# The second mixer of a decoder stack: position bias moved from TensorE to VectorE, heads paired across row halves, GpSimd given half of the normalising, output projection regrouped

## The reference, cut to what matters

```python
proj = h @ w_in            # qa, ka, va | qb, kb, vb | qkv_c, z_c, b_c, a_c
o_a = swa_sink_attention(qa, ka, va, sinks, slopes)   # 4 heads, 2 key heads, window 128, d = 64
o_b = moba_attention(qb, kb, vb, slopes)              # 4 heads, d = 64; causal over all 512 here
#   scores = q.k * d**-0.5 - slope * (distance); masked; softmax (o_a: with a sink term); @ v
o_c = gated_delta_rule(qc, kc, vc, g, beta)           # 4 heads, d = 128, chunks of 64 tokens
#   per chunk: v_new = u - w.S ; o = q.S + a.v_new ; S = S*exp(g_last) + k'.v_new
o_c = rms_norm_2(o_c, dn_norm) * silu(z_c)
mix = concatenate([o_a, o_b, o_c]) @ w_out
x = x + rms_norm_2(mix, mix_post_norm)
```

## Time and profile before

| what | us |
|---|---|
| median of 3 runs (lowest, highest) | 2384.92 (2378.02, 2394.63) |
| the profiled execution | 2380.75 |
| its span, first to last instruction | 2379.0 |
| TensorE busy in the span | 2267.9 (95%) |
| VectorE, ScalarE, GpSimd busy | 1196.2, 894.1, 1055.0 |
| mixer's loop, first score product to the end of the last chunk's work | 1786.9 to 1893.7 |
| mixer's tail, to the first product of the output projection | 1893.7 to 1913.8 |

### The profile page before, as it was taken

How to read it: one execution, slowest core, us unless ns; L and a number is a source line. 1 busy time by engine, 2 the same in 40 slices (tenths; PEclk the granted TensorE clock), 3 DMA queues, 4 the chain that set the end, 5 groups by cost and what they waited for, 6 DMA issues and landing times.

```text
span 2379.0 us, 32320 instructions
## 1 busy us (share of the span) xinstructions
PE 2267.9 (95%) x10448; PEld 1814.8 (76%) x10448; DVE 1196.2 (50%) x1541; ACT 894.1 (38%) x1552; POOL 1055.0 (44%) x785
## 2 busy tenths in 40 slices
PE   7999999999999999999999999989998996999996
PEld 5788888888888786666787788867796664887885
DVE  7822234444432634554248323387774348888613
ACT  4244333443333434443333443334333333323322
POOL 4644445445444445554446544443300032555553
PEclk9999999999999999999999999999999998999998
DMA  3232222222222222111222222222100011232232
GB/s 122 88 106 97 97 91 96 96 97 97 97 97 97 93 97 71 54 54 36 75 86 96 99 95 97 97 94 79 63 10 1 1 62 44 88 100 94 97 106 97
DMA packets 53354, 194.45 MB, mean 82 GB/s; under 512 B 5920, under 2 KB 6176, under 8 KB 53280
## 3 DMA queue, kind: packets, MB, share of 16 engines
q1 hardware_dynamic: 52416, 190.86, 24.1%
q10 hardware_dynamic: 864, 2.59, 0.3%
HBM read 191.34 MB, written 2.10 MB: 81 GB/s over the span
## 4 chain that ended last, share of the span: by engine, by line
PE 44%; issue 36%; POOL 17%; DVE 3%; POOLq 1%; ACT 0%; DVEq 0%; ACTq 0%
POOL w_lo L561 16%; PE proj L619 12%; PE proj L621 12%; PE proj L620 12%; PE aux L764 1%; POOL pr L576 1%; PE proj L789 1%; PE aux L767 1%; PE proj L720 1%; PE proj L718 1%; PE proj L719 1%; DVE act_l L1724 1%; PE aux L775 1%; DVE small L1704 0%; PE proj L746 0%
## 5 line engine op out<-in xcount | busy, mean ns | idle before, releaser
L561 POOL TENSOR_TENSOR w_lo<-w_stage,w_hi 128x512 fp32r<-128x512 f32 x716 | 986.6, 1387 | 1227.3 <-ACT w_hi L1141 1226.7
L1141 ACT ACTIVATE w_hi<-w_stage 128x512 fp32r<-128x512 f32 x716 | 436.7, 627 | 765.4 <-PE proj L621 712.4
L619 PE MATMUL proj<-xh,w_hi 128*128 128x512 f32 x1720 | 683.4, 397 | 36.4 <-POOL w_lo L561 30.6
L620 PE MATMUL proj<-xl,w_hi 128*128 128x512 f32 x1720 | 673.6, 392 | 0.0
L621 PE MATMUL proj<-xh,w_lo 128*128 128x512 f32 x1720 | 673.4, 391 | 0.0
L619 PEld LDWEIGHTS proj<-xh,w_hi 128*128 128x128 f32 x1720 | 324.9, 189 | 125.0 <-POOL w_lo L561 46.3
L621 PEld LDWEIGHTS proj<-xh,w_lo 128*128 128x128 f32 x1720 | 324.7, 189 | 68.3
L620 PEld LDWEIGHTS proj<-xl,w_hi 128*128 128x128 f32 x1720 | 324.8, 189 | 67.7 <-issue 2.5
L619 PE MATMUL proj<-act_h,w_hi 128*128 128x512 f32 (+1 forms) x864 | 337.7, 391 | 0.6 <-POOL w_lo L561 0.6
L620 PE MATMUL proj<-act_l,w_hi 128*128 128x512 f32 (+1 forms) x864 | 337.3, 390 | 0.0
L621 PE MATMUL proj<-act_h,w_lo 128*128 128x512 f32 (+1 forms) x864 | 337.2, 390 | 0.0
(11 more groups left out here) (309 smaller groups left out, 2360.4 us busy)
## 6 DMA issues: line engine op xcount, KB each, us to landing
w_stage<-stream SPq DMA_DIRECT2D x358, 512.0 KB, 3.3
out<-x_res SPq DMA_DIRECT2D x4, 512.0 KB, 2.6
x_res<-x SPq DMA_DIRECT2D x2, 512.0 KB, 5.5
x_res<-x ACTq DMA_DIRECT2D x2, 512.0 KB, 9.5
consts_sb<-consts ACTq DMA_DIRECT2D x1, 832.0 KB, 5.4
pos_i<-pos ACTq DMA_DIRECT2D x1, 256.0 KB, 2.6
consts_sb<-consts ACTq DMA_DIRECT2D x1, 227.0 KB, 6.6
params_sb<-params ACTq DMA_DIRECT2D x1, 194.0 KB, 4.9
```

The lines of the kernel that those rows point to most:

```text
L561: pool.tensor_tensor(w_lo[:, at, :], w_stage[:, at, :], w_hi[:, at, :].bitcast(F32), ALU.subtract).then_inc(stage_free, 1)
L619: pe.matmul(o, w_hi[:, slot, cols], hi, start=(b == 0), stop=False)
L620: pe.matmul(o, w_hi[:, slot, cols], lo, start=False, stop=False)
L1141: act.activation(w_hi[:, u % RING, :], w_stage[:, u % RING, :], ACT.Copy).then_inc(hi_done, 1)
```

## The change

- The bias products and `slope_ident` go. VectorE adds the bias instead: per head one operation in place on the scores in PSUM, distances times minus slope plus score, in front of the row maximum.
- Local heads are paired across key heads, (0, 2) and (1, 3), so that the two lie on opposite row halves; the scores of a pair always take two banks. The rows of the output weight and the sinks are reordered to match.
- `values` goes key block by key block with the two heads inside.
- The scaling is split: VectorE scales head 1 ("nr"), GpSimd head 0 (`pair_scaled`) after the new step "rs". TensorE transposes head 1 first. GpSimd's weight units are cut into those ahead of the pairs and those behind.
- The reciprocal of `r_final` stands ahead of the loop, in the place of `slope_ident`.
- Tiles 0 to 2 of `mixed` are split inside the loop, as soon as their last block is there; tile 3 and the delta tiles behind. Buffers move so that `act_h` is free for it.
- The tail: the square root stands ahead of the last `turn`; the transposes of the norm, the values of pair 14, the spreads, then the values of pair 15.
- The output projection makes its first three tiles side by side, block by block (`together`), then five as before.

```diff
@@ mixer, TensorE
+                        part = slice(64 * t, 64 * t + 64)
+                        q, keys = (a_q[part, tl, :], a_kv[part, 0, :]) if tl < 2 else (b_q[part, tl - 2, :], b_k[part, tl - 2, :])
+                        mm = pe.matmul(pair_scores(k)[:, t, :], q[:, qb * P:qb * P + P], keys[:, first:first + w],
+                                       start=True, stop=True)
-                        pe.matmul(o, q[:, qb * P:qb * P + P], keys[:, first:first + w], start=True, stop=False)
-
-                        mm = pe.matmul(o, slope_ident[:, slope, :], consts2[:, dist - w:dist], start=False, stop=True)
...
-                    for t in range(2):
+                    for t in (1, 0):
+                        if t:
+                            pe.wait_ge(mix_dve, DVE_STEP["nr", k])
+                        else:
+                            pe.wait_ge(pair_scaled, k + 1)
...
-                for t in range(2):
-                    head = 2 * (tl % 2) + t
-                    at = 64 * (head // 2) if tl < 2 else P + 64 * head
-                    for kb_ in range(w // P):
+                for kb_ in range(w // P):
+                    for t, head in enumerate(pair_heads(tl)):
+                        at = 64 * t if tl < 2 else P + 64 * head
...
+                turn(PAIRS)
                 pe.wait_ge(mix_dve, DVE_STEP["orc"])
                 for blk in range(4):
                     mm = pe.transpose(banks(0)[0:4, blk * P:blk * P + P], rc[:, blk * 4:blk * 4 + 4], con("ident", P))
                 made(mm, "ornt")
+                values(PAIRS)
                 pe.wait_ge(mix_dve, DVE_STEP["orn"])
                 for h in HEADS:
                     made(pe.matmul(banks(4 + h), ...), ("ob", h))
+                values(PAIRS + 1)
+                pe.wait_ge(mix_act, ACT_STEP["mc", PAIRS - 1])
...
+                    together(of_act, lambda k: pe.wait_ge(al_done, al.n + k + 1), DT)
+                    for t in range(DT - TOGETHER):
+                        products(tile.n % BANKS, DT, of_act)
@@ mixer, VectorE
-                        link(dve.reciprocal(sums, sums))
-                        for t in range(2):
-                            ins = dve.tensor_scalar(probs[:, n % 2, t, 0:w], probs[:, n % 2, t, 0:w], sums[:, t:t + 1], None, ALU.mult)
-                        made(ins, ("nr", n))
+                        made(dve.reciprocal(sums, sums), ("rs", n))
+                        made(dve.tensor_scalar(probs[:, n % 2, 1, 0:w], probs[:, n % 2, 1, 0:w], sums[:, 1:2], None, ALU.mult), ("nr", n))
...
+                        for t, head in enumerate(pair_heads(tl)):
+                            slope = (SLOPES_SWA if tl < 2 else SLOPES_MOBA)[head]
+                            ins = dve.scalar_tensor_tensor(pair_scores(k)[:, t, :], consts2[:, dist:dist + w], -slope,
+                                                           pair_scores(k)[:, t, :], ALU.mult, ALU.add)
+                        link(ins)
                         link(dve.tensor_reduce(nmax, pair_scores(k), AX.X, ALU.max))
...
                     attend(2 * c + 1)
+                    if c in (3, 5, 7):
+                        lo_of_mixed((c - 3) // 2)
@@ GpSimd
-            lo_units(first, units - first)
+            n = n_units(phases[:phases.index("mixer") + 1]) - RING - 2 * DT + RING
+            lo_units(first, n - first)
+            for k in range(PAIRS):
+                w = pair_of(k)[3]
+                pool.wait_ge(mix_dve, DVE_STEP["rs", k])
+                pool.tensor_scalar(probs[:, k % 2, 0, 0:w], probs[:, k % 2, 0, 0:w], soft[:, k % 2, 1, 0:1], None,
+                                   ALU.mult).then_inc(pair_scaled, 1)
+            lo_units(n, units - n)
```

More of the change, by code:

```diff
@@ L210, in mixer_steps @@
         values(2 * c + 1)
[L211 to L215, removed]
-    act += ["osqrt"]
+    attend(PAIRS)
+    act += ["osqrt"]
+    turn(PAIRS)
+    pe += ["ornt"]
+    values(PAIRS)
+    pe += each("ob")
+    values(PAIRS + 1)
     dve += ["orc", "orn"] + each("on")
@@ L642, in first_tiles @@
                     return
[L643 to L650, removed]
[L651 to L657 removed]
+                together(of_x, lambda k: pe.wait_ge(xl_done, 8 * x_norms[0] + k + 1), DT)
                 stats()
@@ L1073, in hybrid_mixer @@
                     values(2 * c + 1)
-                for k in (PAIRS, PAIRS + 1):
-                    attend(k)
-                    turn(k)
-                    values(k)
+                turn(PAIRS)
                 pe.wait_ge(mix_dve, DVE_STEP["orc"])
@@ L1183, in out_tiles, with grouped_out_tiles_of_y @@
                 deviation(ahead, twice)
+            def grouped_out_tiles_of_y():
+                for t in range(DT):
+                    his(2 * TOGETHER if t == 0 else 2 if t >= TOGETHER else 0)
+                    act.wait_ge(slot_free, unit.now())
+                    square(proj[:, tile.n % BANKS, :])
+                    tile.up()
+                deviation(False)
             def out_tiles_of_y(per_tile):
@@ L1579, in out_tiles, with grouped_out_tiles_of_y @@
                 deviation(twice)
+            def grouped_out_tiles_of_y(post):
+                dve.wait_ge(slot_free, unit.now() + RING + 2 * TOGETHER)
+                for t in range(DT):
+                    b = bank(2)
+                    add_square()
+                    take(dve.tensor_scalar(y[:, t, :], b, par(post, t), None, ALU.mult))
+                deviation()
             def out_tiles_of_y(per_tile, post):
@@ L1906, in hybrid_mixer @@
                                                ALU.subtract), (f"xt{l}", h))
-                for i, slope in enumerate(SLOPES_SWA + SLOPES_MOBA):
-                    ins = dve.tensor_scalar(slope_ident[:, i, :], con("ident", P), -slope, None, ALU.mult)
-                made(ins, "slopes")
+                dve.wait_ge(std_done, stds.n)
+                link(dve.reciprocal(r_final[:, :], r_final[:, :]))
                 def attend(k):
@@ L2166, in weight_blocks @@
             tile(m, P)
+        first_out, w_out = len(out), a["w_out_2"][0]
+        w_out = np.concatenate([w_out[0:64], w_out[128:192], w_out[64:128], w_out[192:]])
         for f in range(DT):
-            tile(a["w_out_2"][0], f * P)
+            tile(w_out, f * P)
+        out[first_out:first_out + TOGETHER * DT] = [out[first_out + i * DT + k] for k in range(DT) for i in range(TOGETHER)]
     if phase == "ffn":
```

113 lines of the change are left out of this document (53 added, 60 removed).

## The result

The changed kernel takes 2369.7 us (median of 5 runs, 2364.2 to 2370.0) against 2384.9 before: ratio 0.9933, interval 0.9909 to 0.9957. The forecast was 2368 in 2354 to 2381; the gain is 15.2 us, forecast 17.3. In the profiled executions the stretch that was forecast, from the loop's first score product to the first product of the output projection, takes 115.7 us against 126.9: 11.2 gained, forecast 17.3. So the total came out closer than the stretch did, and one of the steps behind the forecast did not come out: the clock.

A forecast was written before the change was run, and what follows sets the result against it. TensorE's list bounds the kernel; a ring through four engines replaces it. Loop 90.3 and tail 8.8 us, plus 10.5 for clock and hand-overs, start the output projection 17.3 us earlier: 2384.9 - 17.3 = 2368 us, range 2354 to 2381.

The forecast's parts named there:

- a ring through four engines: Loop: waits through GpSimd, TensorE, VectorE and ScalarE set the pace, 11.3 us a chunk for local heads 256 wide.
- The first two pairs take 11.1: Loop's start: the first two pairs, ahead of chunks 1 to 6, take 11.1 us.
- The start is worth 8: Loop's start: 4 us of TensorE standing and about half of 9.1 us at the lower clock go, 8 us.
- TensorE's own work, 64 us: Loop: its length were TensorE still the bound, 106.8 - 31 - 3.5 - 8 = 64 us.
- The bias at 2 x 0.45: Loop, VectorE: bias on two heads, 0.45 us each, between 0.34 for 128 columns and 0.74 for 512.
- The values, 3.5: Loop, TensorE: values with two heads alternating over opposite column halves save 0 to 8 us, taken as 3.5.
- GpSimd's half is no gain, one engine behind the other: Scaling: GpSimd's 0.93 us against VectorE's 0.35 for 256 columns; one waits for the other, 0.35 on each chunk.
- The tail, 8.8 and 4.5 for the clock: From pair 15's scaling to the output projection: 8.8 us at full clock, plus 4.5 for running at half speed again.
- One or two falls of the clock in the loop, 4 us, and 2 for hand-overs: Loop: TensorE's waits bring one or two clock falls, 4 us; hand-overs not counted elsewhere add 2 us.
- the full-clock sum: Loop: ring links added at full clock put pair 15's scaling 90.3 us after the loop's start.
- what would prove it wrong: Loop: chunks following at 8 us, or at 13 and more, or the clock at half in more than two chunks.
- The rival of the lower clock: Lower clock spreads over the loop: chunks take 16 us, 4.7 more; with all seven 2401 us; chance 4%.

The follow-up runs named there:

- e1: Changed kernel with VectorE scaling the x tile of a chunk after the odd pair's attend instead of before it: 2352.7 us, ratio 0.9862.
- e5: Kernel before with only the reciprocal of r_final moved from chunk 0 to ahead of the loop: 2379.6 us, ratio 0.9983.
- e9: Changed kernel with the bias back on TensorE as products and the x tile scaled after the odd pair's attend: 2351.4 us, ratio 0.9873.
- e10: Changed kernel with the products with the values again going head after head: 2367.7 us, ratio 0.9938.
- e6: Changed kernel with the old tail order, square root, transposes and spreads behind the values of pairs 14 and 15: 2374.2 us, ratio 0.9959.
- e4: Changed kernel with four added products nobody reads on TensorE ahead of the wait for the scaling in all 16 turns: 2355.2 us, ratio 0.9873.
- e2: Changed kernel with the bias back on TensorE as products with a scaled identity: 2362.3 us, ratio 0.9905.
- e7: Changed kernel with x tile late, both heads scaled by VectorE, and scores of pair 2c+1 ahead of values(2c) on TensorE: 2351.5 us, ratio 0.9872.

## Why the prediction was right, and where it was not

- *TensorE's list ceases to be the bound, a ring through four engines takes over*: right. e1 moved 0.75 us a chunk on VectorE alone and shortened the loop by 9.7; the one chunk at full clock took 11.0 us against 11.2, and with the clock at 0.95 pair 15 came at 93.6 against 90.3.
- *The first two pairs take 11.1*: 11.0. *The start is worth 8*: 7.9 up to pair 13 (e5), of which 3.3 reach the end when it is made alone.
- *TensorE's own work, 64 us*: borne out by the 65 us or slightly more of e9 without its bias groups.
- *The bias at 2 x 0.45*: 0.43 for 256 columns, and 0.29 and 0.69 for 128 and 512, a little under the lower bounds of 0.34 and 0.74. The prediction says that no row has the price with PSUM in and out. One did: the mask of the first attention in the kernel before, 256 columns in place, at the 0.43 us that the bias then took.

```profile
L1703 DVE TENSOR_TENSOR aux<-aux,consts_sb 128x256 f32<-128x256 f32 x32 | 13.8, 430 | 69.6 <-PE aux L767 69.1
```

- *The values, 3.5*: real but off the ring (e10), so it was no term of the forecast's end.
- *GpSimd's half is no gain, one engine behind the other*: right in the sum. GpSimd starts 0.06 us after VectorE's scaling starts, not behind it, as the profile shows for pair 15:

```profile
1889.74 0.49 DVE L1951 TENSOR_SCALAR probs<-probs,soft 128x512 f32<-128x512 f32 x1
1889.80 1.86 POOL L600 TENSOR_SCALAR probs<-probs,soft 128x512 f32<-128x512 f32 x1 [6.55 <-DVE soft L1950]
```

  But it takes 1.86 us where it took 1.56 in the first attention, and so ends 1.92 us after VectorE's start. One behind the other would be 0.49 + 1.56 = 2.05, side by side without harm 1.62. By the Trainium skill ("SBUF — State Buffer", Who interferes with whom) one of the two blocks the other for its whole instruction, which would give the 2.05. The trace comes within 0.13 us of that, though the block shows as a longer operation and not as a later start.
- *The tail, 8.8 and 4.5 for the clock*: 14.4 in place of 13.3, 1.1 more; its order is worth 4.2 (e6).
- *One or two falls of the clock in the loop, 4 us, and 2 for hand-overs*: this step failed. Pair 15 came 11.1 us behind the full-clock sum, not 6. The chunks exceed it by 0.5, 2.7, 1.7, 3.1, 2.7, -0.2 and 0.7 us, the first pairs by nothing. The clock fell six times and was at half in parts of more than two chunks, which the prediction had named as what would prove it wrong. The rival of the lower clock had the mechanism and a price of 4.7 us a chunk; at most 3.1 was paid, since no chunk ran at half throughout. What e4 gave back, 7.8 us at a clock of 0.95, is the nearest measure of what the falls cost the loop; the forecast had 4.
- The missing 5 us of the loop and 1.1 of the tail make the first product 6.1 later than forecast (115.7 after the start against 109.6). The gain by the medians is only 2.1 short of the forecast, since the medians of both kernels also carry the 4 us by which the code ahead of the loop varies. That the total came so near is to this extent luck.

So the large edits gave little in this order: of the 11.2 us that the stretch gained (15.2 by the medians), the start and the tail's new order, both small, account for 7.5 to 12. The move of the bias took 5 us of the stretch and 7.5 of the median away again (e2). The pairing of the scores and the early split of `mixed` weren't tried alone, so what each of them is worth stays open.

**A version that beats both.** The changed kernel with the x tile behind the second `attend` (e1), 2352.7, or with the bias left on TensorE as well (e9), 2351.4. By the medians that is 17 to 18 us below the changed kernel and 32 to 33 below the one before; by the stretch, 13 to 16 and 24 to 28. e7 is equal by the median, and its stretch, 97.8, is the shortest.

## What to carry to other kernels

When an engine ceases to be the bound, write down the cycle of waits that takes over and ask of every instruction on it whether it must stand there: 0.75 us of x scaling a chunk, hidden before, cost 13 us of the stretch, while taking 32 products off TensorE brought nothing. And price a gap on TensorE twice, once as time and once as the clock at which all behind it runs; taking work off an engine that then waits can leave its busy time where it was.

## What the runs showed of the hardware that was not expected

- TensorE's clock fell behind short waits: but for the 2.5 us ahead of the last transposes, in which the loop ends, none of the changed kernel's waits in the loop is longer than 2.1 us, and its granted clock is 0.81 there. The sum of standing in the loop doesn't order the kernels by itself. The changed kernel (17.8 us, 0.81), e1 (13.5, 0.86) and e9 (4.4, 1.00) would fit, but e7 (14.9) has 0.90 and e5 (2.8) has 0.95. What else decides, the kind of product or how the waits are spread, no run here separates.
- The clock can fall far from an edit. In e5 the full clock held for 94 us and then fell in the scores of pair 15, behind a wait of 0.69 us. The kernel before has the same wait there, 0.68 us, and kept its clock:

```profile
1881.75 0.44 PE L1039 MATMUL proj<-probs_t,v_tok 128*64 128x128 f32 x4 [0.69 <-ACT mixed L1432]
1882.12 1.38 PE L1008 MATMUL aux<-b_k,b_q 64*128 64x512 f32 x2
1883.42 2.07 PE L1010 MATMUL aux<-consts_sb,slope_ident 128*128 128x512 f32 x2
```

  Why there stays open; no run separates it.
- In the tail of e4 the clock fell from 0.95 to 0.50 while the spread products ran back to back; the last wait of TensorE had ended 7 us earlier. These have four rows (4x512) where the others have 64 or 128. In every kernel the tail ran at 0.50 to 0.83, and this difference, 3 to 4 us of its length, is as large as most edits' effect.

```profile
1888.00:1890.00 2.00, 2.00 (x5) 0.74 (x4) 1.02 (x2) 0.05 (x1) 0.00 (x0) 0.95 0.00 0
1890.00:1892.00 2.00, 2.00 (x4) 0.65 (x2) 0.42 (x1) 0.00 (x0) 0.00 (x0) 0.50 0.00 0
```
